# Experts 0 and 1: picked rows in contiguous slices, their gate and up weights in rows k*128+p

## The reference, cut to what matters

```python
gprob = softmax(xt @ wg + bg);  gp, gidx = top_k(gprob, 1)            # 4 groups
elog  = (xt @ we + be)[group gidx];  ep, eidx = top_k(softmax(elog), 2)  # 8 experts a group
# each (token, expert) pair, weight gp * ep / sum(ep):
hdn = silu(xb @ w_gate[e]) * (xb @ w_up[e])     # (1024 x 512) each
y   = hdn @ w_down[e]                           # (512 x 1024)
out[token] += weight * y
```

## Time and profile before

| | us |
|---|---|
| median of 3 runs | 1782.45 |
| lowest and highest | 1782.27, 1783.71 |
| profiled execution | 1788.86 |
| its span | 1787.0 |
| PE busy in the span | 1574.4 (88%) |
| VectorE busy | 568.5 (32%) |
| mean granted clock of TensorE | 0.972 |

### The profile page before, as it was taken

The page is one execution under the profiler, slowest core; times in us unless marked ns, Lnnn a source line. Parts: engine busy times, 40 slices in busy tenths (PEclk is TensorE's granted clock), DMA queues, the critical chain, the costliest instruction groups (busy, mean ns, idle before and its releaser), DMA issues.

```text
span 1787.0 us, 22127 instructions
## 1 busy us (share of the span) xinstructions
PE 1574.4 (88%) x9144; PEld 957.7 (54%) x9144; DVE 568.5 (32%) x1294; ACT 291.3 (16%) x706; POOL 158.8 (9%) x175
## 2 busy tenths in 40 slices
PE   7999989999799888777699999999998997987783
PEld 3445766566565454444344557664755564544441
DVE  2165246444121111221422742464432211113115
ACT  3131265220000000000123123451100000000001
POOL 0010000002211111110000100000031110111000
PEclk9999999999999999999899999899999999999997
DMA  9103012548999999999821111026599999999994
GB/s 323 68 35 103 8 48 95 196 198 364 425 423 424 424 424 425 422 424 418 362 96 79 53 59 48 1 95 247 224 376 425 424 424 424 423 424 423 424 418 196
DMA packets 72711, 486.57 MB, mean 272 GB/s; under 512 B 24413, under 2 KB 26397, under 8 KB 37792
## 3 DMA queue, kind: packets, MB, share of 16 engines
q1 hardware_dynamic: 62240, 468.81, 63.9%
q0 software_dynamic: 10368, 16.30, 2.5%
HBM read 472.24 MB, written 30.21 MB: 281 GB/s over the span
## 4 chain that ended last, share of the span: by engine, by line
PE 59%; DMA 29%; DVE 4%; SPq 3%; issue 2%; ACT 2%; POOL 1%; DVEq 0%; POOLq 0%; ACTq 0%
DMA RING<-in_w_up 15%; PE banks L623 13%; PE banks L972 11%; PE banks L612 6%; PE banks L925 5%; PE banks L987 5%; DMA TOK<-in_w_up 4%; DMA RING<-in_w_down 3%; DMA TOK<-in_w_gate 2%; PE banks L950 2%; SPq L491 2%; PE banks L849 2%; PE banks L821 1%; DMA XS<-x_rows,SOLVE 1%; PE banks L965 1%
## 5 line engine op out<-in xcount | busy, mean ns | idle before, releaser
L972 PE MATMUL banks<-RING,XS 128*64 128x256 f32 x2752 | 316.5, 385 | 55.1 <-DMA RING<-in_w_up 35.1
L972 PEld LDWEIGHTS banks<-RING,XS 128*64 128x64 f32 x2752 | 218.3, 138 | 164.8 <-DMA RING<-in_w_up 45.1
L623 PE MATMUL banks<-RING,XNT 128*128 128x512 f32 x512 | 226.0, 599 | 0.2 <-DMA RING<-in_w_in_blocks 0.2
L987 PE MATMUL banks<-RING,XS 128*64 128x512 f32 x768 | 177.4, 603 | 27.3 <-issue 13.5
L1808 DVE SCALAR_TENSOR_TENSOR XS<-banks,TABLE,XS 128x256 f32<-128x256 f32 x58 | 28.1, 484 | 435.8 <-PE banks L972 435.8
L623 PEld LDWEIGHTS banks<-RING,XNT 128*128 128x128 f32 x512 | 97.3, 192 | 118.8 <-issue 117.6
L1286 ACT ACTIVATE XS<-banks,TABLE 128x256 f32<-128x256 f32 x58 | 27.4, 473 | 797.2 <-PE banks L972 797.2
L987 PEld LDWEIGHTS banks<-RING,XS 128*64 128x64 f32 x768 | 60.9, 138 | 111.1 <-issue 111.1
L1850 DVE COPY XS<-banks 128x512 f32<-128x512 f32 x64 | 44.2, 691 | 215.6 <-PE banks L987 190.4
L2026 POOL DMA_INDIRECT y_rows<-XS,SOLVE x64 | 65.2, 1019 | 526.4 <-DVE XS L1850 504.4
L612 PE MATMUL banks<-XNT,RING 128*128 128x512 f32 x256 | 110.2, 592 | 0.0
(11 more groups left out here) (346 smaller groups left out, 1756.8 us busy)
## 6 DMA issues: line engine op xcount, KB each, us to landing
RING<-in_w_down SPq DMA_DIRECT2D x46, 2048.0 KB, 27.3
RING<-in_w_up SPq DMA_DIRECT2D x44, 2048.0 KB, 27.5
RING<-in_w_gate SPq DMA_DIRECT2D x42, 2048.0 KB, 27.0
RING<-in_w_in_blocks SPq DMA_DIRECT2D x12, 2048.0 KB, 10.1
TOK<-in_w_gate SPq DMA_DIRECT2D x12, 2048.0 KB, 32.8
TOK<-in_w_up SPq DMA_DIRECT2D x10, 2048.0 KB, 33.2
XNT<-in_w_down SPq DMA_DIRECT2D x8, 2048.0 KB, 30.9
TOK<-in_w_down SPq DMA_DIRECT2D x6, 2048.0 KB, 24.2
```

Source lines behind the costliest of these rows:

```text
L623: last = mm(bank[:, :], XNT[:, k, i * P:(i + 1) * P], w[:, k, :], start=(k == 0), stop=(k == KD - 1))
L972: last = mm(bank[f * CAP:(f + 1) * CAP, 0:256], rows[:, k, :], w[:, k, f * 256:(f + 1) * 256], start=(k == 0), stop=(k == KD - 1))
L987: last = mm(PS[5][n * CAP:(n + 1) * CAP, :], HT[:, j, f * CAP:(f + 1) * CAP], w[:, k, n * BN:(n + 1) * BN], start=(k == 0), stop=(k == KF ...
```

## The change

Two views of the gate and up weights are added, "(k p) f -> p k f": partition p holds rows p, 128 + p, 256 + p and so on, eight pieces of 2 KB in DRAM, 256 KB apart. The loads of gate and up of experts 0 and 1 use them (q // 3 < 2 and q % 3 < 2, four loads a layer). pick_rows takes its stationary operand as 128 neighbouring channels, X3[:, i, k*128:(k+1)*128]. The two copies behind it take the norm2 factors from the channel table PCs, in which partition p has the factors of channels k*128 + p, and no longer from G2K.

```diff
+        wg_kp = w_gate.rearrange("l e (k p) f -> (l e) p k f", p=P)
+        wu_kp = w_up.rearrange("l e (k p) f -> (l e) p k f", p=P)
...
+                    def load_picked(e, m, dst, full):
+
+                        sp.dma_start(dst.rearrange("p (k n) -> p k n", k=KD), (wg_kp, wu_kp)[m][e + layer * NE]).then_inc(full, 16)
...
-                        load(q // 3 if e is None else e, q % 3, TILE[p], tile_full[p])
+                        if q // 3 < 2 and q % 3 < 2:
+                            load_picked(q // 3, q % 3, TILE[p], tile_full[p])
+                        else:
+                            load(q // 3 if e is None else e, q % 3, TILE[p], tile_full[p])
...
-                                last = mm(PS[k // 4][:, (k % 4) * P:(k % 4 + 1) * P], X3[:, i, :].rearrange("t (p k) -> t p k", k=KD)[:, :, k],
+                                last = mm(PS[k // 4][:, (k % 4) * P:(k % 4 + 1) * P], X3[:, i, k * P:(k + 1) * P],
                                           HOT[:, i, :], start=(i == 0 and k % 4 == 0), stop=(i == NT - 1 and k % 4 == 3))
...
+                    def copy_picked(k0, k1):
+                        k = k1 - k0
+                        lo = PC["g2"][0]
+                        return V.tensor_tensor(XT[:, k0:k1, :], PSALL[:, k0 * P:k1 * P].rearrange("p (k s) -> p k s", k=k),
+                                               PCs[:, lo + k0:lo + k1][:, :, None].to_broadcast([P, k, P]), ALU.mult)
...
-                    copy_rows(0, 4, P)
+                    copy_picked(0, 4)
                     dve.wait_ge(*at(layer, picked, 2))
-                    copy_rows(4, 8, P).then_inc(xt_copied, 1)
+                    copy_picked(4, 8).then_inc(xt_copied, 1)
```

## The result

The changed kernel takes 1773.45 us (median of 20 runs, 1765.21 to 1781.39) where the kernel before took 1782.49 us on the same chip (20 runs, 1778.65 to 1790.37). The ratio is 0.9947, with a 95% interval of 0.9933 to 0.9960: 9.0 us less by the medians (0.5%, clear of the noise), where 8.0 were forecast. The profiled execution took 1772.87 us (span 1771.1).

A forecast was written before the change was run, and what follows sets the result against it. The DMA stream was taken to bound the expert stages, with an idle hole in each layer. Closing both holes (10.0 us) less small pieces (2.0 us) gives 8.0 us off 1782.45: 1774.4 us, range 1771.0 to 1781.0.

The forecast's parts named there:

- What bounds the stage: Expert stage: DMA stream sets its end; idle holes ahead of the full stretch, 10.0 us over two layers, count in full.
- The pace of the picking: Row picking on PE: neighbouring reads give 111 ns an instruction, 3.6 us a half in place of 7.7.
- PE's wait for the late ranks: After half 0 of the picking, PE waits 1.9 us for DVE's second set of choices.
- How much reaches expert 0: Picking to expert 0's first product: expert 0 starts 6.4 us earlier, load for tile 0 issued at 408.3, not 414.70.
- its first rival: Clock dips at PE's waits, or the next hand-over, take back 1 to 2.5 us a layer; gain 3 to 6 us; chance 0.22.
- the slack of 2.3 us: Ahead of the closed hole: tile 0's load has 2.3 us in hand; one dip, 1.6 us, fits within it.
- The copies: Two copies behind the picking, factors from another table: no cost, no gain, 0.69 us each.
- The small pieces: Expert 1's gate and up loads in 2 KB pieces: 0.5 us more a tile, four tiles, 2.0 us in all.
- The sum: Whole kernel: 10.0 us from the holes less 2.0 us for the pieces gives 8.0 us of gain.
- The signs: Changed profile, among others: no DVE wait for picking over 1 us, DMA share 1.0, expert 1's loads at least 395 GB/s.
- SyncE: Load queue: handing out eight times the pieces is covered; over 18 us would delay tile 0's load and reopen the hole.
- The next hand-over: Load at 470.07, waiting for PE behind the next gather: a hole opens if the gather is not 4 us earlier.

The follow-up runs named there:

- experiment 7: Changed kernel with sixteen spare products right ahead of expert 0's first product; 1777.59 us, ratio 0.9965 to the kernel before.
- experiments 2 and 4: First: see experiment 2. Second: changed kernel with expert 1's gate and up loads exchanged with expert 2's up and gate; 1773.62 us, ratio 0.9947.
- experiment 2: Changed kernel with gate and up of experts 0 and 1 loaded in 16 KB pieces from a host-laid-out copy; 1773.29 us, ratio 0.9948.

## Why the prediction was right, step by step

**What bounds the stage** was read rightly. The hole was the price: closing it gave 8.8 us by the stage, and experiment 7 reopened it. Its size was read too small: the two holes were worth 11.4 us by the bytes, where the forecast took 10.0 from the busy shares.

**The pace of the picking.** 3.6 us a half were forecast from L702, 3.84 measured (start to modelled end; 32 instructions at 111 ns are 3.6). The reason given, jumps of eight elements, was right in kind and too narrow: jumps of four cost nearly the same.

**PE's wait for the late ranks.** 1.9 us forecast, 1.68 and 1.69 measured.

**How much reaches expert 0.** Layer 2 is as forecast: half 0 to expert 0's first product is 1277.49 - 1264.95 = 12.54 us, where 18.7 less 6.4 is 12.3, and the load for tile 0 goes out 16.25 us behind the start, 16.0 forecast. Layer 1 met the dip that the prediction gave to its first rival: half 1 in a dip takes 6.06 us, the first product comes after 15.22 us and the load after 18.94. I had given a dip 1.6 us, from one of 3.3 us at 1.2 GHz; this one holds the whole half and cost 2.2 us there, and 0.5 us more on the late ranks ahead of it (1.29 us in place of 1.08 for L952, 0.72 in place of 0.44 for L953), so that half 1 starts 8.38 us behind half 0 and not 7.92. So the load came 2.7 us late, and the slack of 2.3 us was used up. The prediction had let one such dip pass for free (1.6 us against 2.3); that term was too small. The dent it left is worth 1.0 us by the bytes. By the stage a dip in layer 1 costs more: 471.56 to 471.82 us in the four traces that have one (the changed kernel twice, experiments 2 and 4), 469.80 to 470.04 in the three with spare products, so 1.5 to 2.0 us. That is the rival's price of 1 to 2.5 us a layer, in one layer of two. DVE was to be the later one at the copies. In layer 2 it was, by a hair: it runs both without a wait. In layer 1, with the dip, it waited 0.86 and 1.51 us for PE (DVE's timeline, layer 1 and then layer 2).

```profile
403.12 0.69 DVE L1811 TENSOR_TENSOR XS<-banks,PCOL 128x512 f32<-128x512 f32 x1 [0.86 <-PE banks L959]
405.33 0.69 DVE L1811 TENSOR_TENSOR XS<-banks,PCOL 128x512 f32<-128x512 f32 x1 [1.51 <-PE banks L959]
```

```profile
1275.93 1.50 DVE L1811 TENSOR_TENSOR XS<-banks,PCOL 128x512 f32<-128x512 f32 x2
```

**The copies.** 0.69 us each in layer 1, as the row of before.

**The small pieces.** 0.5 us a tile was forecast and 0.46 to 0.50 measured. Giving this back brought nothing (experiments 2 and 4), because with larger pieces the queue runs dry earlier and the stream loses in both layers what the pieces save.

**The sum.** By the bytes the stream got back 11.4 - 1.2 = 10.2 us at the holes and paid 2.0 us for the pieces: 8.2 us, where the stage gives 8.8 and the forecast was 8.0. So the mechanism held, and the closeness of the number is in part luck: holes read 1.4 us too small stand against a dip that was taken to be free and left 1.0 us.

**The signs.** Three of those named ahead did not come out in full. DVE waited more than 1 us for the picking in layer 1 (1.51). The share was not 1.0 throughout (0.89 in 410 to 412 us), though it stayed over 0.9 in 5 us. The stretch in which expert 1's tiles are carried ran at 390 GB/s (398 to 404 us), a little under the 395 that were named.

**SyncE.** The prediction said that handing out the small pieces is covered unless it takes over 18 us. It was held for 2.50 us at L491 and 7.05 us at the load behind it; in experiment 2 the same two rows are 1.36 us for the pair and 0.47. The next load is wanted 12 us later, so it is covered.

**The next hand-over.** The load that stood at 470.07 stands at 464.81, 5.3 us earlier, or 3.8 against the start of the picking, and the window up to 475 us has a share of 1.01. No hole opened.

## What to carry to other kernels

Read which resource has holes in an otherwise full stretch, and ask which one event ends the hole; work ahead of that event counts at full rate until the hole is closed and at little from there on, so a second saving of the same kind is worth trying only for what is left of it. Measure the hole by the bytes that are missing and not by the busy share: here the share read 10.0 us where 11.4 were lost, and it showed 0.99 where the stream was thin. Shortening the stream itself (larger pieces) moves the moment at which it runs dry, and can open the hole again: here it brought nothing. In this kernel a stationary operand read with a step of four or eight float32 elements cost twice the time of one read with a step of one or two; if the contraction or output order is free, move the stride into the layout of the other operand, where here it cost 0.5 us a tile in DMA pieces. Compare traces over the stage that the change touches, from one of its events to another, since what lay between the two stages moved a single pair of profiles by 6.2 us, two thirds of the change.

## What the hardware showed beyond the forecast

- The step of a stationary float32 read has a cliff, not a slope: the 32 matmul instructions of a half (16 products) with their weight loads take 3.84, 4.04, 7.73 and 7.88 us at steps 1, 2, 4 and 8.
- At step 8 the pace did not follow the clock (7.88 and 7.92 us, the second partly at a granted clock of 0.58); at step 1 a half took 3.84 us at 1.00 and 6.06 us at 0.51.
- A tile of 2 MB in 2 KB pieces costs 0.46 to 0.50 us more than in 16 KB pieces (399 against 424 GB/s over a stretch in which two tiles of three are small).
- Behind a hole the stream starts slowly: 119, 348 and 475 GB/s in the three microseconds from 415 to 418 us of the kernel before. The busy share of the same window, hole and restart together, understates the loss.
- A load of 1024 pieces holds the queue that issues it once others are under way: 0.84 us for the first, 2.50 us for the second, and 7.05 us for the load behind them, against 0.33 us for a load of 16 KB pieces into an empty queue.
- Around the same waits of 1.7 and 1.0 us on PE the clock fell to 0.51 in layer 1 and stayed at 1.00 in layer 2 of one execution of the changed kernel. Half 1 of layer 1 was struck in all six traces that have this picking without spare products at step 1 (5.47 to 6.11 us). In the trace of step 2 half 1 was struck in layer 2 alone (5.57 us there, 4.04 in layer 1), in that of the delayed expert 0 in both layers; in the three traces with spare products in the waits in neither.
